# Layer norms of a two-layer decoder trunk: the shift added by ScalarE, the sums and folds written as scalar_tensor_tensor

## The reference, cut to what matters

```python
def layer_norm(x, g, b):
    xf = x.astype(jnp.float32)
    mu = jnp.mean(xf, axis=-1, keepdims=True)
    var = jnp.mean(jnp.square(xf - mu), axis=-1, keepdims=True)
    return ((xf - mu) * lax.rsqrt(var + LN_EPS) * g + b).astype(x.dtype)
...
def swiglu(x, w_gu, w_down):
    gu = x @ w_gu
    return (jax.nn.silu(gu[..., :D_FF]) * gu[..., D_FF:]) @ w_down
...
        yp = layer_norm(DN_ALPHA * yp + mp, ln_g[i, 0], ln_b[i, 0])
        yp = layer_norm(DN_ALPHA * yp + swiglu(yp, ffn_w_gu[i], ffn_w_down[i]), ln_g[i, 1], ln_b[i, 1])
```

## Time and profile before

| | us |
|---|---|
| median of three executions | 1948.25 |
| lowest, highest | 1944.16, 1948.9 |
| the profiled execution, its own time | 1947.65 |
| its span | 1945.9 |
| PE busy in the span | 1711.2 (88%) |
| DVE, ACT, POOL busy | 634.3, 549.9, 733.9 |

### The profile page before, as it was taken

The page is one execution under the profiler, slowest core; times in us unless marked ns, Lnnn a source line. Parts: engine busy times, 40 slices in busy tenths (PEclk is TensorE's granted clock), DMA queues, the critical chain, the costliest instruction groups (busy, mean ns, idle before and its releaser), DMA issues. The chain is left out here.

```text
span 1945.9 us, 37991 instructions
## 1 busy us (share of the span) xinstructions
PE 1711.2 (88%) x15074; PEld 1557.6 (80%) x15074; DVE 634.3 (33%) x1282; ACT 549.9 (28%) x1064; POOL 733.9 (38%) x532
## 2 busy tenths in 40 slices
PE   4699279996988896899999999898998899999996
PEld 4599269864665665899999999897666899999996
DVE  1211101034444553751111116515564831111127
ACT  1222000002554443343132222304442442222211
POOL 3551203132333544654434433622114564344420
PEclk8799589977999998999999999899888899999998
DMA  6521666703553552333233332213503333323201
GB/s 223 167 74 45 169 202 210 230 12 95 182 160 110 164 171 70 108 98 109 88 88 92 93 88 66 76 47 97 173 1 109 88 108 88 95 79 103 86 20 45
DMA packets 296181, 210.54 MB, mean 108 GB/s; under 512 B 33934, under 2 KB 289220, under 8 KB 295492
## 3 DMA queue, kind: packets, MB, share of 16 engines
q1 hardware_dynamic: 275212, 163.65, 28.8%
q10 hardware_dynamic: 12136, 23.09, 3.7%
q0 software_dynamic: 8656, 21.37, 3.6%
HBM read 197.97 MB, written 18.42 MB: 111 GB/s over the span
## 5 line engine op out<-in xcount | busy, mean ns | idle before, releaser
L1572 PE MATMUL ps<-x_high,w_high_t 128*128 128x256 f32 (+1 forms) x1488 | 427.2, 287 | 11.1 <-POOL w_low_t L1495 6.6
L1495 POOL TENSOR_TENSOR w_low_t<-w_raw,w_high_t 128x1024 fp32r<-128x1024 f32 (+1 forms) x130 | 308.0, 2378 | 326.0 <-ACT w_high_t L1600 326.0
L1573 PE MATMUL ps<-x_low,w_high_t 128*128 128x256 f32 (+1 forms) x1488 | 423.0, 284 | 0.0
L1574 PE MATMUL ps<-x_high,w_low_t 128*128 128x256 f32 (+1 forms) x1488 | 422.5, 284 | 0.0
L1572 PEld LDWEIGHTS ps<-x_high,w_high_t 128*128 128x128 f32 x1488 | 283.4, 190 | 15.0 <-POOL x_low L1505 7.8
L1573 PEld LDWEIGHTS ps<-x_low,w_high_t 128*128 128x128 f32 x1488 | 283.2, 190 | 0.3
L1574 PEld LDWEIGHTS ps<-x_high,w_low_t 128*128 128x128 f32 x1488 | 282.7, 190 | 0.0
L551 PE MATMUL ps<-rows,w 64*64 64x128 f32 (+2 forms) x2048 | 152.6, 481 | 49.7 <-DMA rows<-in_cache_cmp 49.7
L551 PEld LDWEIGHTS ps<-rows,w 64*64 64x64 f32 x2048 | 132.4, 159 | 69.4 <-issue 49.9
L1600 ACT CAST w_high_t<-w_raw 128x1024 fp32r<-128x1024 f32 (+1 forms) x130 | 132.1, 1025 | 146.6 <-PE ps L1574 123.5
L1684 DVE TENSOR_TENSOR h_t<-silu_t,ps 128x256 f32<-128x256 f32 (+1 forms) x88 | 37.4, 425 | 359.0 <-PE ps L1574 354.6
(11 more groups left out here) (337 smaller groups left out, 3279.9 us busy)
## 6 DMA issues: line engine op xcount, KB each, us to landing
w_raw<-in_ffn_w_gu SPq DMA_DIRECT2D x88, 512.0 KB, 3.8
pages<-in_cache_slc SPq DMA_DIRECT2D x192, 128.0 KB
w_raw<-in_ffn_w_down SPq DMA_DIRECT2D x32, 448.0 KB, 3.6
rows<-in_cache_cmp SPq DMA_DIRECT2D x104, 128.0 KB, 4.9
w_raw<-in_gla_w_in SPq DMA_DIRECT2D x24, 512.0 KB, 3.6
rows<-in_cache_cmp ACTq DMA_DIRECT2D x80, 128.0 KB, 5.6
rows<-in_cache_cmp POOLq DMA_DIRECT2D x72, 128.0 KB, 4.6
pages<-in_cache_slc POOLq DMA_DIRECT2D x64, 128.0 KB, 2.6
```

The lines of the kernel that those rows point to most:

```text
L1495: nc.gpsimd.tensor_tensor(low(u)[:, 0:k], raw[:, u % RAW, 0:k], high(u)[:, 0:k].bitcast(F32), ALU.subtract).then_inc(low_done, 1)
L1572: nc.tensor.matmul(psum(i), high(u)[:, k, :], a[0][:, at, c], start=(k == 0), stop=False)
L1573: nc.tensor.matmul(psum(i), high(u)[:, k, :], a[1][:, at, c], start=False, stop=False)
L1574: ins = nc.tensor.matmul(psum(i), low(u)[:, k, :], a[0][:, at, c], start=False, stop=(k == t.kc - 1))
```

## The change

Three edits, all in `phase_trunk`:

1. The shift of a layer norm (L1738, a `tensor_scalar` add on DVE, 8 per norm, 64 in all) is dropped there and becomes an `activation` Identity with the shift as bias on ACT (new function `shift_of`), in place on `xT`. DVE's multiply now signals a new semaphore `scaled`, for which ACT waits. ACT does shift k, then the high part of k - 1.
2. The running sum (L1704, 56 in all) becomes a `scalar_tensor_tensor` with scalar 1.0, (a * 1.0) + b.
3. The three folds (L1717, 24 in all) likewise.

```diff
@@ ScalarE
+            def shift_of(n, k):
+                x = xT[:, k, cols(norms[n][1])]
+                act.wait_ge(scaled, n * KT + k + 1)
+                nc.scalar.activation(x, x, ACT.Identity, bias=shift(n)[:, k:k + 1]).then_inc(normed, 1)
+
...
                     if store is not None and n >= NNORM - 2:
+                        for k in range(KT):
+                            shift_of(n, k)
                         continue
-                    for k in range(KT):
-                        act.wait_ge(normed, n * KT + k + 1)
-                        nc.scalar.copy(X[0][:, k, c], xT[:, k, c]).then_inc(xh_done, 1)
+                    for k in range(KT + 1):
+                        if k < KT:
+                            shift_of(n, k)
+                        if k:
+                            act.wait_ge(normed, n * KT + k)
+                            nc.scalar.copy(X[0][:, k - 1, c], xT[:, k - 1, c]).then_inc(xh_done, 1)
@@ VectorE
-                        nc.vector.tensor_tensor(total[:, hf, 0:w], xT[:, 0, c] if t.m == 1 else total[:, hf, 0:w], x,
-                                                ALU.add).then_inc(sum_done, 1)
+                        nc.vector.scalar_tensor_tensor(out=total[:, hf, 0:w],
+                                                       in0=xT[:, 0, c] if t.m == 1 else total[:, hf, 0:w], scalar=1.0,
+                                                       in1=x, op0=ALU.mult, op1=ALU.add).then_inc(sum_done, 1)
...
-                        nc.vector.tensor_tensor(sq[:, 0:half, 0:w], sq[:, 0:half, 0:w], sq[:, half:2 * half, 0:w],
-                                                ALU.add).then_inc(folded, 1)
+                        nc.vector.scalar_tensor_tensor(out=sq[:, 0:half, 0:w], in0=sq[:, 0:half, 0:w], scalar=1.0,
+                                                       in1=sq[:, half:2 * half, 0:w], op0=ALU.mult, op1=ALU.add)\
+                            .then_inc(folded, 1)
...
-                    for k in range(KT + 1):
-                        if k < KT:
-                            x = xT[:, k, c]
-                            ins = nc.vector.scalar_tensor_tensor(out=x, in0=x, scalar=gain(n)[:, k:k + 1],
-                                                                 in1=sd[:, 0:w], op0=ALU.mult, op1=ALU.mult)
-                            own += 1
-                            ins.then_inc(dve_own, 1)
-                        if k:
-                            dve.wait_ge(dve_own, own - (k < KT))
-                            x = xT[:, k - 1, c]
-                            nc.vector.tensor_scalar(x, x, shift(n)[:, k - 1:k], None, ALU.add).then_inc(normed, 1)
+                    for k in range(KT):
+                        x = xT[:, k, c]
+                        nc.vector.scalar_tensor_tensor(out=x, in0=x, scalar=gain(n)[:, k:k + 1], in1=sd[:, 0:w],
+                                                       op0=ALU.mult, op1=ALU.mult).then_inc(scaled, 1)
```

More of the change, by code:

```diff
@@ L1415, in phase_trunk @@
         dve_own = sem("dve_own")
-        sum_done, mean_done, centred, squared, folded, var_done, std_done, normed, xh_done, xl_done = (
+        sum_done, mean_done, centred, squared, folded, var_done, std_done, scaled, normed, xh_done, xl_done = (
             sem(n) for n in ("ln_sum", "ln_mean", "ln_centred", "ln_squared", "ln_folded", "ln_var", "ln_std",
-                             "ln_normed", "x_high", "x_low"))
+                             "ln_scaled", "ln_normed", "x_high", "x_low"))
         tr_done, tr_act, tr_dve, y_out = sem("ytr"), sem("ytr_act"), sem("ytr_dve"), sem("y_out")
```

## The result

The changed kernel takes 1929.74 us (median of six executions, 1927.26 to 1931.46) against 1948.38 for the kernel before (six, 1944.16 to 1949.13): a ratio of 0.9909, 95% interval 0.9898 to 0.992. That is 18.6 us, where 20 were forecast. The profiled execution has a span of 1928.2 us, 17.7 less than before.

The account below looks back on a forecast made before the run. PE, busy 88%, bounds the kernel, so only its layer-norm waits count. Gains 6.7 + 6.7 + 6.7 + 1.6 = 21.7 us, less 1.6 for the clock, leave 20.1: 1928 us, range 1921 to 1941.

Parts of the forecast that it names:

- Edits 2 and 3 at nothing: Running sums and folds in the new form: same cost, same turns with POOL, so 0 us gained.
- place 1: t0's first layer norm: shift on ACT starts the second half's variance at 834.5 instead of 840.56, 6.1 us, plus 0.6.
- Place 2: t0's layer norm at 1203 to 1236 us: second half's variance near 1229.8 instead of 1236.5, 6.7 us gained.
- Place 3: The layer norm in t1, written by the same code: place 1 over again, 6.7 us gained.
- Place 4: The very end, PE waiting for last shifts and transposes: last shift at 1936.1 instead of 1937.71, 1.6 us gained.
- The clock: Half clock behind the new 2.4 us variance waits at place 1 and Place 3: one of two counted, 1.6 us back.
- the later fresh pass: Pass on the second half's normed tiles: small waits for x_low go, between 0.4 and 0.8 us, taken as 0.6.
- (a): Rival: new sums and folds do not wait for POOL; about 37 us gained, 1911 us, chance 0.07.
- (b): Rival: new form runs at half rate on two SBUF tensors; 8 us slower, 1956 us, chance 0.04.
- (c): Rival: second half's variance waits over 2.4 us behind w_lows, clock at 0.50; 8 to 12 gained, 1938, chance 0.17.
- (d): Rival: ACT sets the pace or a hidden semaphore wait eats the gain; within 3 us of before, chance 0.03.
- The first signs: Mean's wait under 1 us, about 2 us at second half's variance under w_low, shift 0.49 us, end 5.7 us.

Follow-up runs that it names:

- the second experiment: Kernel before with only the running sums and folds as scalar_tensor_tensor, the shift left on VectorE: 1947.45 us, ratio 1.0005.

## Why the prediction was right

**Edits 2 and 3 at nothing: right, and shown.** The kernel with them alone is 1.0005 of before. The row that carried this was the multiply held up at 815.62. The Trainium skill's sentence that this form halves its rate with two SBUF sources that aren't bf16 ("Vector Engine (DVE) Microarchitecture Reference", "Points that are easy to get wrong") does not hold here: both forms take 424 ns at the least at 256 columns.

**Edit 1 at place 1: right step by step.** Counted from the first multiply, forecast and measured: last sum ends 8.1 and 8.3 us behind it, the mean 9.1 and 9.4, POOL's last w_low ends 18.2 and 18.5, the variance starts 20.6 and 20.85, where it started 26.67 before. The gain is 5.8, forecast 6.1. The shift took 507 ns at the median (forecast 0.49), and ScalarE's pair 0.71 apart, as forecast. The new wait at the variance is 2.35 us by its row, forecast 2.4.

**Place 2:** from the first multiply (1206.80) to the variance 20.4 us, before 26.7: 6.3 gained, forecast 6.7. Its new wait is 1.92, forecast 1.4. PE is there 18.5 us behind the first multiply, as I had said (18.6), but the last w_low ends 19.3 us behind it and not 18.2. Here two folds in turn meet a w_low (3.48 and 2.77 us long), and the last w_low in its turn waits for the first fold.

**Place 3** repeats place 1, as was assumed from the code: the wait there is 2.38 us at 1533.37. **Place 4:** the last transposes start 7.6 us behind the variance matmul (1920.04 less 1912.46), before 9.2 (1937.76 less 1928.61): 1.6, as forecast.

**The clock is the term that was mis-sized.** I counted one of the two new waits of 2.4 us as costing 1.6 us. Both did: behind 836.68 and 1533.37 the clock stood at 0.50 for 3.3 us, which cost 1.7 and 1.5 us against the kernel before. The sum in the two traces is 5.82 + 6.29 + 6.05 us up to the variance at places 1 to 3, 0.8 each at the later fresh pass of places 1 and 3 (forecast 0.6), 1.57 at place 4, less 3.3 for the clock (0.1 of it at place 2): 18.0 us, against 20.1. The upper level behind the first half's variance at place 2 put PE 1.4 us ahead of the kernel before, but the fresh pass waited for x_low all the same, so nothing of that counts. So 1.7 of the 2.1 us missing are the clock, and 0.7 are the variances of places 1 and 2, with 0.4 more than forecast at the fresh passes. The spans differ by 17.7, as t0 starts 1.9 us later in the changed kernel's execution and the linear attention between the calls is 1.6 us shorter. The second experiment's kernel, which leaves the shift where it was, has it 2.9 us shorter than the kernel before, so this is no work of the change.

**The rivals.** (a) and (b) fell with the second experiment. (c) had the right queue, but the waits at the variance stayed at 1.9 to 2.4 us, as four w_low are all that are queued. (d) fell with the extra copies on ScalarE. The first signs that I had listed all came: no wait at the means, a wait of about 2 us at the variance under POOL's w_low, 507 ns for the shift. From the last reciprocal (1914.26) to the last transposes it takes 5.8 us, where I had 5.7.

## What to carry to other kernels

Before you make a chain on one engine shorter, write down what the other engines have queued at the time to which it moves up: here 4.3 us of wait at the mean, with some 2 us of clock behind it, turned into 2.4 us of wait one step on, at the variance, behind queued work that nobody was waiting for yet. Work with slack that holds a resource of the late step (here POOL's w_low and DVE's folds) can be worth a wait of its own, 15 us here for two waits per layer norm; but follow what that work releases, since the same idea taken two passes further cost 20 us through a load buffer. Rewriting an instruction in another form that reads the same two tensors moved nothing here; look first for a row of the form you mean to change to that meets the same trouble.

## What the runs showed of the hardware

**VectorE and GpSimd take turns.** With both reading SBUF, VectorE with two inputs there, eight x_low and the DVE work between them alternate one for one in these traces: x_low 0.88 us apart with a turn between, 0.74 long without one. A 1056-column fold, 1.26 us by itself, takes 3.44 to 3.48 where it meets a w_low of 2.4: it waits for one, and in none of these traces for two. The subtraction of the mean, which has one of its inputs in PSUM, does not wait (1.26 and 1.25 us from 1216.83 on, under w_low; 1.25 at 1906.37, where GpSimd has nothing to do).

**The same wait does not always cost the clock.** The granted clock of four stretches right behind a wait at the variance, two of the changed kernel (waits of 2.35 and 2.51 us) and then two of the kernel with the extra copies (2.56 us each). Columns: stretch, us, busy (xinstructions) of PE, PEld, DVE, ACT, POOL, clock, DMA share, GB/s.

```profile
836.80:840.10 3.30, 3.30 (x14) 3.09 (x15) 1.46 (x3) 2.17 (x3) 0.00 (x0) 0.50 0.21 63
1200.20:1203.60 3.40, 3.40 (x27) 3.35 (x28) 3.33 (x4) 0.48 (x1) 3.40 (x2) 1.00 0.62 168
```

```profile
838.60:842.00 3.40, 2.99 (x23) 2.92 (x24) 1.56 (x4) 2.17 (x3) 0.00 (x0) 1.00 0.40 119
1535.50:1538.90 3.40, 3.32 (x26) 3.26 (x27) 1.56 (x4) 2.17 (x3) 0.00 (x0) 1.00 0.26 78
```

The shorter wait was followed by the lower level (1.2 GHz), the three longer ones by the upper (2.4 GHz); in the kernel before, the 2.51 us at 1203 were followed by the lower level too. It is not the chance of one execution: the kernel with edit 1 alone has the levels of the changed kernel (0.52 behind 2.40 us, 1.00 behind 2.52, 0.59 behind 2.35), and the one with edits 2 and 3 alone has the level of the kernel before (0.52 behind 2.52 us at 1206). What tells the places apart is left open. For a forecast it means that a wait of 2 to 3 us may or may not cost another 1.5.
